# Expert blocks of 32 rows in four column groups of TensorE, turned by VectorE, with the down part one block behind

## The chip, the cores and the metric

The kernel runs on one core of one Trainium2 chip. The metric is the device time of one execution in microseconds (us). Three runs of the kernel before took 1458.22, 1455.94 and 1453.58 us, median 1455.94. One execution more was recorded by the profiler; its rows are read below. In them PE is TensorE's matmul, PEld its weight load, DVE is VectorE, ACT ScalarE, POOL GpSimd and SP SyncE, which here issues the weight loads. A "q" behind an engine's name is its sequencer.

## The reference

One step of a hybrid backbone on 512 sample and 128 prompt tokens, model width 1024, all in f32: a norm and modulation, two token mixers (an S5 scan and a gated linear recurrence), an output projection, then a mixture of 16 experts with two experts per token, and a final norm. The change is in the mixture of experts alone:

```python
    def expert_block(args):
        xe, e = args
        return (jax.nn.silu(xe @ w_gate[e]) * (xe @ w_up[e])) @ w_down[e]

    yb = lax.map(expert_block, (xb.reshape(n_blocks, MOE_BLOCK, dm), blk_expert)).reshape(-1, dm)
    y_slot = yb[dest] * wts.reshape(-1)[order][:, None].astype(x.dtype)
    return jax.ops.segment_sum(y_slot, tok, num_segments=n_tok)
```

640 tokens x 2 = 1280 rows are sorted by expert. Every expert's rows are padded to whole blocks. Each expert has three matrices of 1024 x 1024 f32, 4 MB each, 192 MB in all, and each is read once from HBM.

## The kernel before, in words

Everything up to the router (slices 1 to 21 of 40) keeps its order. From there on the program is a pipeline over blocks of MB = 64 sorted rows.

- **Routing.** VectorE counts the rows per expert, orders the experts and writes block numbers into `router_ints` (lines 1495 to 1610). Expert 0 comes first, since its weights can be loaded before the router is known; the others alternate between the largest and the smallest that are left. GpSimd scatters the rows of `h2` to `x_sorted` in HBM (L659). The first block's rows are picked by matmul (L2241) instead and need no trip through HBM.
- **PE, one block** (the loop at lines 2268 to 2294). The stationary operand is 64 columns of turned x; the weights are streamed, 256 or 512 columns at a time, in two column groups of the array side by side. `gates(s)`, eight times, does gate and up (L2222); `down(f)`, eight times, the last product (L2233). PE turns x of the next block (`turn_x`, L2212) and the activations (`turn_act`, L2228) itself, by matmul with an identity, in the middle of these. The down part of a block follows its own gate part. The trace counts two records per f32 matmul.
- **ScalarE** takes silu of the gate half (L948), copies turned activations (L951) and turned x (L936) out of PSUM, loads x of the block after next (L956) and stores y (L973). **VectorE** multiplies by the up half (L1661) and copies y (L1682).
- **Weights.** An expert is 24 pieces of 512 KB, each with a slot of its own in SBUF. SP issues the loads in a fixed order (`next_expert`, L525 to L553). For each expert 10 of the 16 gate and up pieces go to ten staging buffers (L532) and are copied by GpSimd into their slots when the last block of the expert before has used these (L673). The other six go straight to their slots behind waits on `gu_done` (L542, L544), the eight down pieces behind waits on `down_done` (L553). The last expert is loaded without staging.
- **The end.** y of all blocks but the last two comes back by gathers from `y_sorted` (L685) and is scaled and added by VectorE (L1643, L1647). The last two blocks stay in SBUF (`y_last`, L1656) and are merged by matmuls with `last_tokens_t` (L2311).

## Time and profile before

| | |
|---|---|
| median of three runs | 1455.94 us |
| span of the profiled execution | 1449.7 us |
| what lies around the span, median less span | 6.2 us |
| PE busy | 1358.5 us, 94% |
| PE weight load busy | 850.3 us, 59% |
| VectorE, ScalarE, GpSimd busy | 433.9, 265.5, 234.1 us |
| chain that ended last | PE 79%, DMA 8%, VectorE 5% |
| moved by DMA | 318.07 MB, mean 219 GB/s |

Each of the 40 slices is 36.2 us. A digit is the busy share in tenths. PE's share alone does not say whether the expert stage waits for weights; the steps of SP's loads from expert to expert and the DMA share of a stretch do.

### The profile page before, as it was taken

Reading aid. Unit: us, or ns where it says so; the run is one execution under the profiler, and the core shown is the slowest. Engines: PE = TensorE matmul, PEld = TensorE weight load, DVE = VectorE, ACT = ScalarE, POOL = GpSimd, SP = SyncE. Lnnn points to the kernel's source line nnn. Section 1 sums busy time; section 2 is a strip of 40 time slices with the busy share of each in tenths; the row PEclk is TensorE's granted clock in tenths of the full one; section 3 lists DMA queues with packets and bytes.
Section 4 is the critical chain, followed back from the end, with each engine's and each line's share of the span. In section 5 each row is a group of like instructions: output and inputs, shape, how many; then the busy total and the mean of one; then the engine's idle time right before and its main releaser. Section 6 shows DMA issues by size and latency. Waiting matters only on the chain.

```text
span 1449.7 us, 26021 instructions
## 1 busy us (share of the span) xinstructions
PE 1358.5 (94%) x10242; PEld 850.3 (59%) x10243; DVE 433.9 (30%) x913; ACT 265.5 (18%) x401; POOL 234.1 (16%) x280
## 2 busy tenths in 40 slices
PE   5898999978999999999969999999999999999975
PEld 3688778756787666664434455555555455554532
DVE  4792860375622412104462000000000000000065
ACT  3305012244125000000111111111111111111102
POOL 0043402200000000000005013003122222222320
PEclk9899899998999999999989999999999999999997
DMA  7459622345430212413168818917949999999993
GB/s 302 152 136 386 140 69 66 81 147 181 170 111 10 87 44 73 172 46 145 44 249 330 342 29 340 395 29 292 396 155 396 389 398 380 403 380 403 377 402 132
DMA packets 91756, 318.07 MB, mean 219 GB/s; under 512 B 11920, under 2 KB 12304, under 8 KB 91440
## 3 DMA queue, kind: packets, MB, share of 16 engines
q1 hardware_dynamic: 72304, 268.77, 48.9%
q0 software_dynamic: 10608, 34.19, 8.0%
q10 hardware_dynamic: 8784, 14.24, 3.2%
q8 instruction: 46, 0.75, 0.2%
q14 instruction: 14, 0.11, 0.0%
HBM read 281.99 MB, written 33.06 MB: 217 GB/s over the span
## 4 chain that ended last, share of the span: by engine, by line
PE 79%; DMA 8%; DVE 5%; issue 3%; ACT 2%; SPq 2%; POOL 0%; POOLq 0%; DVEq 0%; ACTq 0%
PE ps L2222 22%; PE ps L1762 11%; PE ps L2233 11%; PE ps L1750 10%; DMA expert_w<-in_w_down 5%; PE ps L2132 5%; PE ps L2183 4%; PE ps L1854 2%; PE ps L1937 2%; DMA expert_w<-in_w_up 2%; SPq L553 1%; PE ps L2228 1%; PE ps L2212 1%; PE ps L1777 1%; DMA x_sorted<-h,router_ints 1%
## 5 line engine op out<-in xcount | busy, mean ns | idle before, releaser
L2222 PE MATMUL ps<-expert_w,x_block_t 128*64 128x256 f32 x3584 | 405.8, 383 | 10.6 <-issue 6.7
L2222 PEld LDWEIGHTS ps<-expert_w,x_block_t 128*64 128x64 f32 x3584 | 257.2, 138 | 159.1 <-issue 33.7
L2233 PE MATMUL ps<-expert_w,act_t 128*64 128x512 f32 x896 | 212.7, 602 | 4.1 <-DMA expert_w<-in_w_down 3.7
L1762 PE MATMUL ps<-h_t,weight_ring 128*128 128x320 f32 x640 | 179.0, 436 | 0.1
L1762 PEld LDWEIGHTS ps<-h_t,weight_ring 128*128 128x128 f32 x640 | 121.6, 191 | 54.2 <-issue 7.6
L1750 PE MATMUL ps<-h_t,weight_ring 128*128 128x320 f32 x512 | 148.8, 454 | 2.8 <-ACT h_t L730 2.8
L1661 DVE TENSOR_TENSOR activations<-silu_tmp,ps 128x256 f32<-128x256 f32 x56 | 23.6, 422 | 375.7 <-ACT silu_tmp L948 375.6
L1750 PEld LDWEIGHTS ps<-h_t,weight_ring 128*128 128x128 f32 x512 | 102.0, 201 | 46.7 <-issue 9.3
L2233 PEld LDWEIGHTS ps<-expert_w,act_t 128*64 128x64 f32 x896 | 58.3, 137 | 101.4 <-issue 81.4
L673 POOL COPY expert_w<-staged 128x1024 f32<-128x1024 f32 x42 | 43.8, 1043 | 416.8 <-PE ps L2222 315.9
L1682 DVE COPY y_block<-ps 128x512 f32<-128x512 f32 x25 | 17.3, 692 | 187.5 <-PE ps L2233 187.5
L2183 PE MATMUL ps<-w_out_sb,merged 128*128 128x512 f32 x160 | 71.1, 597 | 0.7 <-DVE x L1479 0.7
L948 ACT ACTIVATE silu_tmp<-ps 128x256 f32<-128x256 f32 x56 | 21.6, 385 | 243.3 <-PE ps L2222 234.9
L659 POOL DMA_INDIRECT x_sorted<-h,router_ints x10 | 9.7, 973 | 336.0 <-DVE router_ints L1592 333.2
L673 POOL COPY expert_w<-gathered 128x1024 f32<-128x1024 f32 x56 | 57.9, 1043 | 11.5 <-DMA gathered<-in_w_gate 8.9
L948 ACT ACT_TABLE_LOAD x27 | 34.6, 1283 | 130.8 <-issue 130.8
L2183 PEld LDWEIGHTS ps<-w_out_sb,merged 128*128 128x128 f32 x160 | 29.6, 190 | 37.0 <-issue 33.9
L1777 PE MATMUL ps<-weight_ring,c_silu 128*32 128x128 f32 x768 | 27.4, 290 | 19.4 <-DMA weight_ring<-in_stream 14.7
L704 ACT ACTIVATE gates<-ps 128x640 f32<-128x640 f32 x16 | 11.3, 704 | 169.5 <-PE ps L1762 169.5
L951 ACT ACTIVATE act_t<-ps 128x256 f32<-128x256 f32 x56 | 21.5, 384 | 100.4 <-PE ps L2228 100.4
L1854 PEld LDWEIGHTS ps<-weight_ring,h_t 128*128 128x128 f32 x320 | 35.9, 192 | 0.2
L1854 PE MATMUL ps<-weight_ring,h_t 128*128 128x128 f32 x320 | 35.9, 275 | 0.0
(355 smaller groups left out, 1309.1 us busy)
## 6 DMA issues: line engine op xcount, KB each, us to landing
expert_w<-in_w_down SPq DMA_DIRECT2D x128, 512.0 KB, 13.6
weight_ring<-in_stream SPq DMA_DIRECT2D x98, 512.0 KB, 5.0
expert_w<-in_w_gate SPq DMA_DIRECT2D x58, 512.0 KB, 11.3
expert_w<-in_w_up SPq DMA_DIRECT2D x58, 512.0 KB, 12.3
staged<-in_w_gate SPq DMA_DIRECT2D x28, 512.0 KB, 13.9
gathered<-in_w_gate SPq DMA_DIRECT2D x28, 512.0 KB, 15.9
gathered<-in_w_up SPq DMA_DIRECT2D x28, 512.0 KB, 16.5
x_sorted<-zero POOLq DMA_DIRECT2D x18, 512.0 KB, 15.0
```

What stands on the lines that cost most here:

```text
L673: nc.gpsimd.tensor_copy(w_slot[3 * f + s % 2][:, :, :].rearrange("p k c -> p (k c)"), stage[s])\
L948: nc.scalar.activation(silu[:, a, :], ps[:, 2 * a, 0:256], ACT.Silu).then_inc(silu_ready, 1)
L1661: vec.tensor_tensor(acts[:, a, :], silu[:, a, :], ps[:, 2 * a + 1, 0:256], ALU.mult).then_inc(prod_ready, 1)
L1750: last = mm(pair(job)[:, a, :], w[:, k, :], h_t[:, k, a * HALF:(a + 1) * HALF], start=(k == 0), stop=(k == KD - 1))
L1762: last = mm(pair(job)[:, a, :], w[:, k, :], h_t[:, k, a * HALF:(a + 1) * HALF], start=(k == 0), stop=(k == KD - 1))
L1777: last = mm(pair_flat(job)[rows, 0, j * P:(j + 1) * P], csil[:, k, :], w[:, k, :], start=(k < 4), stop=(k >= 4))
L1854: last = mm(pair_flat(job)[:, 0, m * P:(m + 1) * P], h_t[:, k, c * P:(c + 1) * P], ring[:, slots[m], k, :], start=(k == 0), stop=(k == KD ...
L1937: last = mm(pair(job)[:, g2, i * NB + lo:i * NB + hi], lhs, rhs, start=False, stop=(i == 3 and ri == 1 and lo > 0), skip_group_check=True)
L2132: last = mm(bank(job)[:, 0:HALF], br[:, 4 * w + k, :], y[:, k, a * HALF:(a + 1) * HALF], start=(k == 0), stop=(k == 3))
L2183: last = mm(bank(job), merged[:, k, c * P:(c + 1) * P], wo[:, k, 512 * half:512 * half + 512], start=(k == 0), stop=(k == KD - 1))
L2222: last = mm(ps[MB * g:MB * g + MB, 2 * half + w, 0:256], x_blk_t[:, 2 * kp + k2, :], rows[:, at_col:at_col + 256], start=(kp == 0 and k2 = ...
L2233: last = mm(ps[MB * half:MB * half + MB, 4, :], act_t[:, 4 * (f // 4) + 2 * (f % 2) + f // 2 % 2, :], w_slot[3 * f + 2][:, 4 * half:4 * ha ...
```

## The change

A block has 32 rows. Gate and up weights are laid out so that a piece holds, for one slice of 128 of the contraction, four strips of 256 columns (128 of up, 128 of gate); four matmuls of 32 stationary columns, one per column group, stream one strip each. The down product is cut the same way. x and the activations lie on 4 x 32 partitions, and VectorE turns them with a transpose within squares of 32; PE turns nothing in the loop. The down part of a block runs behind the gate part of the next block. All 16 gate and up pieces of every expert but the first pass through 8 staging buffers and a copy of GpSimd, with the last expert no exception; the down pieces go straight to their slots. The last four blocks stay in SBUF. With these inputs the rows per expert, in the kernel's order of experts, are 61, 209, 26, 204, 29, 134, 33, 108, 36, 88, 39, 85, 49, 65, 56 and 58.

```diff
@@ -58,14 +58,19 @@
 TILE = 32
 
 EXPERTS, EGROUPS, EPG = 16, 4, 4
-MB = 64
+MB = 32
 OVER = (2 * TOK - EXPERTS) // MB
 NBLK = EXPERTS + OVER
 X_ROWS = (NBLK + 2) * MB
 Y_ROWS = NBLK * MB
 DFF = 1024
 KF = DFF // P
-STAGED = 10
+FG = 4
+GW = D // FG
+LASTN = 4
+STAGES = 8
+PIECES = 3 * KF
...
+        w_slot = [at(f"expert_w{s}", end - s * 4096, [P, D]) for s in range(PIECES)]
+        piece = [w_slot[n] for n in SLOT_OF]
...
+        stage = [at("staged0", end + 4096, [P, D])[:, :], sm[:, b_at:b_at + D]] \
+            + [at(f"staged{2 + i}", ring0 + 12288 + i * 4096, [P, D])[:, :] for i in range(3)] \
+            + [at(f"staged{5 + i}", qs0 + 5632 + i * 4096, [P, D])[:, :] for i in range(3)]
...
             first_expert(range(20, 24))
-            def next_expert(n, staged):
+            def load_piece(e, p):
+                sp.dma_start(stage[p % STAGES], w_experts[bass.ds(e, 1), p, :, :].rearrange("a p n -> p (a n)"))\
+                    .then_inc(stage_in[p % STAGES], 16)
+
+            sp.wait_ge(act_took, h2_job("L", CH - 1) + 1)
+            sp.wait_ge(route_ready, 1)
+            second = sp.value_load(rint[0:1, EXPERT + 1:EXPERT + 2], min_val=0, max_val=EXPERTS - 1)
+            for p in range(STAGES // 2):
+                load_piece(second, p)
+            sp.wait_ge(x_scattered, 16 * 2 * CH)
+            for g in range(FG):
+                sp.dma_start(x_blk[MB * g:MB * g + MB, :], x_sorted[MB:2 * MB, GW * g:GW * g + GW]).then_inc(x_blk_in, 16)
+            def load_down(b, e):
+                for f in range(KF):
+                    sp.wait_ge(down_done, b * KF + (f + 1))
+                    sp.dma_start(piece[2 * KF + f][:, :], w_experts[bass.ds(e, 1), 2 * KF + f, :, :].rearrange("a p n -> p (a n)"))\
+                        .then_inc(down_in[f], 16)
+
+            for p in range(STAGES // 2, 2 * KF):
+                if p >= STAGES:
+                    sp.wait_ge(slot_filled, 2 * KF + (p + 1 - STAGES))
+                load_piece(second, p)
+            load_down(sp.value_load(rint[0:1, START + 1:START + 2], min_val=0, max_val=NBLK), second)
+            with sp.Fori(2, EXPERTS) as n:
                 b = sp.value_load(rint[0:1, bass.ds(n + START, 1)], min_val=0, max_val=NBLK)
                 e = sp.value_load(rint[0:1, bass.ds(n + EXPERT, 1)], min_val=0, max_val=EXPERTS - 1)
...
+                for p in range(2 * KF):
+                    sp.wait_ge(slot_filled, n * (2 * KF) + (p + 1 - STAGES))
+                    load_piece(e, p)
+                load_down(b, e)
...
-            pool.sem_inc(slot_filled, STAGED)
+            for p in range(2 * KF):
+                pool.wait_ge(first_in[p], 16)
+            pool.sem_inc(slot_filled, 2 * KF)
             pool.wait_ge(route_ready, 1)
-            with pool.Fori(1, EXPERTS - 1) as n:
+            with pool.Fori(1, EXPERTS) as n:
                 b = pool.value_load(rint[0:1, bass.ds(n + START, 1)], min_val=0, max_val=NBLK)
...
+                for p in range(2 * KF):
+                    s = p % STAGES
+                    pool.wait_ge(stage_in[s], n * (16 * 2 * KF // STAGES) + 16 * (p // STAGES + 1 - 2 * KF // STAGES))
                     pool.sem_inc(stage_full, 1)
...
+                    pool.wait_ge(gu_done, b * (2 * KF) + (p + 1))
+                    pool.sem_inc(slot_free, 1)
+                    nc.gpsimd.tensor_copy(piece[p][:, :], stage[s]).then_inc(slot_filled, 1)
...
+            with act.Fori(2, NBLK) as i:
+                with act.If(i < limit):
+                    for h in range(2):
+                        act.wait_ge(gu_done, i * (2 * KF) + (h + 1) * KF)
+                        act.wait_ge(prod_ready, i * 2 + h)
+                        take_gate_half(h)
+                    act.wait_ge(xt_copied, i + 2)
                     load_x(i * MB + 2 * MB)
...
+                    act.wait_ge(y_copied, i + 1)
+                    store_y(i * MB - MB)
...
+            dve.wait_ge(picked0, 1)
+            vec.transpose(x_blk_t[:, :, :].rearrange("p k t -> p (k t)"), ps[:, 5, 0:GW]).then_inc(xt_copied, 1)
...
+            def take_prod(h):
+                vec.tensor_tensor(acts[:, h, :], silu[:, :], ps[:, h, 0:P], ALU.mult).then_inc(prod_ready, 1)
+
+            def turn_x(src):
+                vec.transpose(x_blk_t[:, :, :].rearrange("p k t -> p (k t)"), src).then_inc(xt_copied, 1)
+
+            def turn_act():
+                vec.transpose(act_t[:, :, :].rearrange("p k t -> p (k t)"), acts[:, :, :].rearrange("p h n -> p (h n)"))\
+                    .then_inc(act_ready, 1)
+
+            def copy_y():
+                vec.tensor_copy(y_blk[:, :], ps[:, 4, 0:GW]).then_inc(y_copied, 1)
+
+            for i in range(2):
+                dve.wait_ge(silu_ready, 2 * i + 1)
+                take_prod(0)
+                dve.wait_ge(silu_ready, 2 * i + 2)
+                take_prod(1)
+                dve.wait_ge(prod_ready, 2 * i + 2)
+                if i == 1:
+                    dve.wait_ge(down_done, KF)
+                turn_act()
+                if i == 0:
+                    last_picks()
+                dve.wait_ge(x_blk_in, (i + 1) * 16 * FG)
+                dve.wait_ge(gu_done, (i + 1) * 2 * KF)
+                turn_x(x_blk[:, :])
+                if i == 0:
+                    dve.wait_ge(down_done, KF)
+                    dve.wait_ge(y_stored, 16 * FG)
+                    copy_y()
+            with dve.Fori(2, NBLK) as i:
+                with dve.If(i < limit):
+                    dve.wait_ge(silu_ready, i * 2 + 1)
+                    take_prod(0)
+                    dve.wait_ge(x_blk_in, i * (16 * FG) + 16 * FG)
+                    dve.wait_ge(gu_done, i * (2 * KF) + 2 * KF)
+                    turn_x(x_blk[:, :])
+                    dve.wait_ge(silu_ready, i * 2 + 2)
+                    take_prod(1)
+                    dve.wait_ge(prod_ready, i * 2 + 2)
+                    dve.wait_ge(down_done, i * KF)
+                    turn_act()
+                    dve.wait_ge(y_stored, i * (16 * FG))
+                    copy_y()
...
+            def gate_half(h, filled):
+                for k in range(KD):
+                    filled(KD * h + k)
+                    for g in range(FG):
+                        last = mm(ps[MB * g:MB * g + MB, h, 0:GW], x_blk_t[:, k, :], piece[KD * h + k][:, GW * g:GW * g + GW],
+                                  start=(k == 0), stop=(k == KD - 1))
+                    last.then_inc(gu_done, 1)
+
+            def down(filled):
+                for f in range(KF):
+                    filled(2 * KD + f)
+                    for g in range(FG):
+                        last = mm(ps[MB * g:MB * g + MB, 4, 0:GW], act_t[:, f, :], piece[2 * KD + f][:, GW * g:GW * g + GW],
+                                  start=(f == 0), stop=(f == KF - 1))
+                    last.then_inc(down_done, 1)
...
             blocks = pe.value_load(rint[0:1, TOTAL:TOTAL + 1], min_val=EXPERTS, max_val=NBLK)
-            with pe.Fori(1, NBLK) as i:
+            own = pe.value_load(rint[0:1, 1:2], min_val=0, max_val=EXPERTS - 1)
+            pe.wait_ge(xt_copied, 2)
+            gate_half(0, lambda p: pe.wait_ge(slot_filled, own * (2 * KF) + (p + 1)))
+            pe.wait_ge(prod_ready, 2)
+            gate_half(1, lambda p: pe.wait_ge(slot_filled, own * (2 * KF) + (p + 1)))
+            with pe.Fori(2, NBLK) as i:
                 with pe.If(i < blocks):
                     e = pe.value_load(rint[0:1, bass.ds(i, 1)], min_val=0, max_val=EXPERTS - 1)
+                    before = pe.value_load(rint[0:1, bass.ds(i - 1, 1)], min_val=0, max_val=EXPERTS - 1)
                     pe.wait_ge(xt_copied, i + 1)
...
+                    gate_half(0, lambda p: pe.wait_ge(slot_filled, e * (2 * KF) + (p + 1)))
+                    pe.wait_ge(prod_ready, i * 2)
+                    gate_half(1, lambda p: pe.wait_ge(slot_filled, e * (2 * KF) + (p + 1)))
+                    pe.wait_ge(act_ready, i)
+                    pe.wait_ge(y_copied, i)
+                    down(lambda p: pe.wait_ge(down_in[p - 2 * KF], before * 16 + 16))
...
+            pe.wait_ge(act_ready, blocks)
+            pe.wait_ge(y_copied, blocks)
+            down(lambda p: pe.wait_ge(down_in[p - 2 * KF], EXPERTS * 16))
...
+    def by_group(w):
+        return w.reshape(EXPERTS, FG, KD, MB, FG, 2, P).transpose(0, 5, 2, 1, 3, 4, 6)
+
+    gate_up = np.stack([by_group(a["moe_w_up"][0]), by_group(a["moe_w_gate"][0])], axis=6).reshape(EXPERTS, 2 * KD, P, D)
+    down = a["moe_w_down"][0].reshape(EXPERTS, FG, KF, MB, D).transpose(0, 2, 1, 3, 4).reshape(EXPERTS, KF, P, D)
```

What it moves on PE. Before, in the loop over blocks: the last gate/up part of a block, then its down part with a turn of the second half of its activations in it.

```order
L2222 MATMUL ps<-expert_w_170,x_block_t 64x256 [waits gu_in7]
L2222 MATMUL ps<-expert_w_170,x_block_t 64x256
L2222 MATMUL ps<-expert_w_171,x_block_t 64x256 x2
L2222 MATMUL ps<-expert_w_170,x_block_t 64x256 x2
L2222 MATMUL ps<-expert_w_171,x_block_t 64x256 x2
L2287 ISA [waits act_ready]
L2233 MATMUL ps<-expert_w_151,act_t 64x512 [waits y_copied,dn_in0]
L2233 MATMUL ps<-expert_w_151,act_t 64x512
L2233 MATMUL ps<-expert_w_154,act_t 64x512 [waits dn_in1]
L2233 MATMUL ps<-expert_w_154,act_t 64x512
L2283 REGISTER_ALU
L2228 MATMUL ps<-constants,activations 128x128 [waits prod_ready]
```

Now, at the same place: the last two gate/up pieces of block i, then the down part of block i - 1.

```order
L2220 MATMUL ps<-expert_w_164,x_block_t 32x256 [waits slot_filled]
L2220 MATMUL ps<-expert_w_164,x_block_t 32x256 x3
L2263 REGISTER_ALU
L2220 MATMUL ps<-expert_w_152,x_block_t 32x256 [waits slot_filled]
L2220 MATMUL ps<-expert_w_152,x_block_t 32x256 x3
L2266 ISA [waits y_copied,act_ready]
L2228 MATMUL ps<-expert_w_153,act_t 32x256 [waits first_in16]
L2228 MATMUL ps<-expert_w_153,act_t 32x256 x3
L2228 MATMUL ps<-expert_w_154,act_t 32x256 [waits first_in17]
L2228 MATMUL ps<-expert_w_154,act_t 32x256 x3
```

The turns are gone from PE, every four matmuls have a wait of their own, and the down part reads the activations of the block before.

SP before, in the loop over experts: the last gate and up pieces wait for the gate part of the expert before (`gu_done`), and the down pieces follow.

```order
L542 DMA expert_w_167<-in_w_gate 128x1024
L544 DMA expert_w_168<-in_w_up 128x1024
L541 REGISTER_ALU
L542 ISA [waits gu_done]
L542 DMA expert_w_170<-in_w_gate 128x1024
L544 DMA expert_w_171<-in_w_up 128x1024
L552 REGISTER_ALU
L553 DMA expert_w_151<-in_w_down 128x1024 [waits down_done]
```

SP now, at the same place (`expert_w_153` is the first down piece):

```order
L525 ISA [waits slot_filled]
L525 DMA staged_188<-in_w_experts 128x1024
L551 REGISTER_ALU
L525 ISA [waits slot_filled]
L525 DMA staged_189<-in_w_experts 128x1024
L538 ISA
L539 ISA [waits down_done]
L539 DMA expert_w_153<-in_w_experts 128x1024
```

All sixteen gate and up loads now wait for copies (`slot_filled`), and `down_done` is the count of a down part that PE runs one block later than before.

## Rows read from the trace of the kernel before

**Rows 1.** Page, part 2: DMA share and GB/s in 40 slices.

```profile
DMA  7459622345430212413168818917949999999993
GB/s 302 152 136 386 140 69 66 81 147 181 170 111 10 87 44 73 172 46 145 44 249 330 342 29 340 395 29 292 396 155 396 389 398 380 403 380 403 377 402 132
```

**Rows 2.** Timeline of PE, one block: start us, us, engine, line, operation.

```profile
862.38 8.80 PE L2222 MATMUL ps<-expert_w,x_block_t 128*64 128x256 f32 x80
871.12 0.44 PE L2228 MATMUL ps<-constants,activations 128*128 128x128 f32 x2
871.49 5.40 PE L2222 MATMUL ps<-expert_w,x_block_t 128*64 128x256 f32 x48
876.72 1.89 PE L2233 MATMUL ps<-expert_w,act_t 128*64 128x512 f32 x8
...
878.90 2.80 PE L2233 MATMUL ps<-expert_w,act_t 128*64 128x512 f32 x12
881.63 0.66 PE L2212 MATMUL ps<-constants,x_block 128*128 128x128 f32 x4
...
884.84 8.80 PE L2222 MATMUL ps<-expert_w,x_block_t 128*64 128x256 f32 x80
```

**Rows 3.** Timeline of SP's queue: loads of down pieces for the next expert.

```profile
792.06 9.48 SPq L553 DMA_DIRECT2D expert_w<-in_w_down  x8
878.06 7.33 SPq L553 DMA_DIRECT2D expert_w<-in_w_down  x8
903.04 12.03 SPq L553 DMA_DIRECT2D expert_w<-in_w_down  x8
...
1394.04 8.62 SPq L553 DMA_DIRECT2D expert_w<-in_w_down  x8
```

**Rows 4.** Windows: stretch, its us, busy us by engine, PEclk, DMA share, GB/s.

```profile
1240.00:1248.00 8.00, 8.00 (x43) 2.78 (x40) 0.57 (x2) 0.99 (x3) 6.58 (x7) 1.00 1.03 410
1107.00:1175.00 68.00, 67.43 (x506) 36.04 (x504) 4.60 (x9) 10.26 (x18) 20.59 (x20) 1.00 1.02 393
```

**Rows 5.** Timeline of PE: four column groups, in the conditioning stage.

```profile
410.69 1.95 PE L1777 MATMUL ps<-weight_ring,c_silu 128*32 128x128 f32 x64
```

**Rows 6.** Page, part 3: ScalarE's DMA queue, packets, MB, share of 16 engines.

```profile
q10 hardware_dynamic: 8784, 14.24, 3.2%
```

**Rows 7.** Page, part 5: GpSimd's copies, busy and mean ns, idle before.

```profile
L673 POOL COPY expert_w<-staged 128x1024 f32<-128x1024 f32 x42 | 43.8, 1043 | 416.8 <-PE ps L2222 315.9
```

**Rows 8.** Timeline of SP's queue, after a stretch in which nothing was loaded.

```profile
873.68 0.33 SPq L542 DMA_DIRECT2D expert_w<-in_w_gate  x1
```

**Rows 9.** Windows around that issue.

```profile
870.00:874.50 4.50, 4.50 (x42) 2.78 (x40) 0.35 (x1) 0.39 (x1) 4.37 (x5) 1.00 0.00 0
874.50:876.00 1.50, 1.50 (x18) 1.00 (x14) 0.00 (x0) 0.00 (x0) 0.00 (x0) 1.00 0.81 295
```

**Rows 10.** Windows: stretches before and after a change of PE's granted clock.

```profile
743.00:757.00 14.00, 7.06 (x18) 2.83 (x20) 12.34 (x50) 0.00 (x0) 0.00 (x0) 0.52 1.03 411
1399.00:1405.00 6.00, 4.85 (x22) 2.73 (x24) 4.71 (x5) 0.39 (x1) 0.86 (x1) 0.50 1.02 409
1411.00:1416.00 5.00, 2.26 (x10) 0.50 (x12) 1.86 (x2) 0.05 (x1) 0.00 (x0) 0.99 1.03 409
1416.00:1419.00 3.00, 3.00 (x10) 1.06 (x12) 2.93 (x3) 0.04 (x1) 0.00 (x0) 0.50 0.73 289
```

**Rows 11.** Timeline of SP's queue: the load of the second block's rows.

```profile
783.49 1.19 SPq L565 DMA_DIRECT2D x_block<-x_sorted  x2
```

**Rows 12.** Timeline of VectorE: a scaling, the last block, the first merged chunks.

```profile
1381.98 2.48 DVE L1643 SCALAR_TENSOR_TENSOR gathered<-gathered,router_tiles,gate_row 128x1024 f32<-128x1024 f32 x2 [3.32 <-DMA gathered<-y_sorted,router_ints]
1421.89 2.81 DVE L1656 TENSOR_TENSOR y_last<-ps,gate_row 64x512 f32<-64x512 f32 x4 [2.75 <-PE ps L2233]
1433.19 2.35 DVE L1707 TENSOR_TENSOR final<-ps,x 128x1024 f32<-128x1024 f32 x2 [8.49 <-PE ps L2311]
```

**Rows 13.** Timeline of ScalarE's queue: the load of one block's rows.

```profile
1313.71 1.20 ACTq L956 DMA_DIRECT2D x_block<-x_sorted  x2
```

More of the change, by code:

```diff
@@ L244, in hybrid_step @@
+        got = [at(f"gathered{i}", qs0 + 20480 + i * 4096, [P, D])[:, :] for i in range(3)]
+        y_last = at("y_last", qs0 + 20480 + 3 * 4096, [P, 2, D])
         b_at = SMALL["b_re"][0]
[L245 to L247 removed]
@@ L325, in hybrid_step @@
         blocks_done = sem("blocks_done")
-        got_in = [sem(f"got_in{s}") for s in range(CH)]
+        got_in = [sem(f"got_in{s}") for s in range(3)]
         pick_ready = sem("pick_ready")
@@ L1648, in add_gathered @@
-                if part == 3:
+                                                  g2_row[:, 0 if c < SCH else 1, :], ALU.mult, ALU.mult))
+                else:
+                    settle()
+                    steps[0] += 1
+                    vec.tensor_tensor(x2[:, c, :], x2[:, c, :], row, ALU.add).then_inc(dve_step, 1)
                     settle()
                     vec.nop().then_inc(got_used, 1)
-            def take_last(u, cv):
-                for half in range(2):
-                    rows = slice(MB * half, MB * half + MB)
-                    last = vec.tensor_tensor(y_last[rows, u, cv, :], ps[rows, 4, :],
-                                             g2_row[rows, cv, 512 * half:512 * half + 512], ALU.mult)
-                last.then_inc(y_last_ready, 1)
```

415 lines of the change are left out of this document (129 added, 286 removed).

## Prediction

> **What bounds the kernel now.** I read the slices first [rows 1]. From slice 22 (761 us) on it is the expert stage. Its first nine slices show DMA digits between 1 and 9 with 29 to 396 GB/s, the next nine 9s with 377 to 403. So the DMA engines have slack early and none late. PE's own rows say what sets the pace early [rows 2]: a block of 64 tokens runs from 862.38 to 884.84, 22.46 us, and PE does not wait in it. SP's first load of each expert's down weights marks the step from expert to expert [rows 3]. It comes at 792.06 for the second expert and at 1394.04 for the sixteenth: 602.0 us for 14 experts. They hold 26 of the 28 blocks, 26 x 22.46 = 584 us, so PE is the limit for 97% of that stage. An expert with four blocks takes 86.0 us (792.06 to 878.06), one with one block 25.0 (to 903.04), which is less than its weights need on the DMA engines: they were fetched ahead. A pair with three blocks then takes 68 us at 393 GB/s [rows 4], where PE (67.4) and 48 pieces of weights nearly balance.
>
> **PE per block.** A gate/up record (64 columns, 256 streamed, two groups) costs (876.72 - 862.38 - 0.37 for the turn) / 128 = 109 ns, a down record (881.63 - 878.90) / 12 = 227 ns of 512 [rows 2]. With four groups half of each per 256 columns is left if all four run together: 54.6 and 57 ns. The one place with four groups today streams 128 columns, 64 records in 1.95 us [rows 5], 30.5 ns each, so they do run together. A block of 32 has 128 gate/up and 64 down records: 7.0 + 3.6 = 10.6 us. Bounds: 10.2 if the rate is exactly that of the two-group records without their gaps, 11.7 if 256 columns cost twice the 30.5. I take 10.6, from the nearer shapes. The PE transposes (2 x 0.37 + 0.59 us a block) go. No VectorE transpose stands in the trace. Its bounds are 0.35 us (VectorE takes 0.69 for 512 columns out of PSUM [rows 12], this is 256) and, in four passes, 1.4; turning x lies beside the down part one block behind (3.6 us), turning the activations beside the next gate part, so I take nothing. If one took over 3.6 us it would show 48 times.
>
> **Blocks.** Routing the given inputs with the reference gives, in the kernel's order of experts, 61, 209, 26, 204, 29, 134, 33, 108, 36, 88, 39, 85, 49, 65, 56, 58 rows. In 32s that is 2, 7, 1, 7, 1, 5, 2, 4, 2, 3, 2, 3, 2, 3, 2, 2: 48 blocks for 28. PE alone would need 48 x 10.6 = 509 us instead of 629. That is the saving on offer, 120 us.
>
> **The weights.** They stay 24 pieces of 512 KB an expert. Undisturbed the engines move 410 GB/s [rows 4]: 1.28 us a piece, 30.7 an expert. ScalarE's queue (x and y blocks) took 3.2% of the span [rows 6], 46.4 us or 1.66 for each old block of 256 packets of 2 KB. A new block has 256 packets of 1 KB: between 0.83 (by bytes) and 1.66 (by packets), I take 1.2.
>
> **The new wait.** This is the term that decides. SP issues in order: 16 gate/up pieces of expert n, then 8 down pieces, each behind a wait for the down part of the last block of expert n-1. That part now runs one block behind, after the gate/up of expert n's first block, which needs all 16 pieces. So the last staged piece must land, be copied and be used before SP may issue anything, the next expert's pieces are queued behind it, and the DMA engines run dry once per expert. The price: copy 1.04 us [rows 7]; landing and two signals 0.4; eight gate/up records 0.44; eight down records 0.44; and 1.1 from SP's issue at 873.68 [rows 8] to the first bytes (the share is 0.00 until 874.5 and 0.81 in the 1.5 us after [rows 9]). Sum 3.4 us. Those 16 records run at half clock, for in the 1.28 us between pieces PE has work for 0.44: after the stretch 1411 to 1416, in which PE waited for pieces and was busy 2.26 of 5 us, the granted clock was 0.50 [rows 10], the 1.2 GHz level. That adds 0.9: 4.3 us. Bounds: 0 (if the engines never run dry) and 6.
>
> The Trainium skill (TensorE: Matmul & The Clock Gate, "HAM oscillation — how this bites in real kernels") says that a matmul stream broken by waits for DMA is throttled again at each wait, and it speaks against splitting this work into smaller pieces. The rows above agree; without that rule the sum would be 19 us less, with it taken to the letter 22 more, both among the rivals.
>
> So an expert that is bound by its weights takes 30.7 + 4.3 + 1.2 per block: 36.2 us with one block, 37.4 with two, 38.6 with three. With four or more PE is the longer: 10.6 per block, plus 2.6 for the about 5 us at half clock until a full stream has raised it (743 to 757 was 14 us at 0.52, 1399 to 1405 six us at 0.50 [rows 10]): 45.0, 55.6 and 76.8 us for 4, 5 and 7. Only 8 pieces are staged, so after a long expert the next 16 still have to come. The sum for the second to the fifteenth expert: 2 x 36.2 + 5 x 37.4 + 3 x 38.6 + 45.0 + 55.6 + 2 x 76.8 = 629.4 us, against 602.0: **+27.4**.
>
> **Where it starts.** SP waits until the rows are scattered and asks for the second block at 783.49 [rows 11]; the engines moved 411 GB/s before that [rows 10], so this stays. Today the second block is a full one of 22.46 and SP's first down load comes at 792.06, during it. Afterwards: x lands about 787.5, gate/up of block 1 (7.0 + 2.6 at half clock) to 797, gate/up of block 2 to 805, down load at 806. The 16 pieces are there by 804 (12 of them from 786 on, 15.4 us, then a copy). **+14.0**. The first block starts some 5 us sooner, since no PE transpose and ScalarE copy stand before it, but it then waits for that x anyhow. The routing arithmetic grows by 20 block slots, under 1 us, hidden by the scatter's DMA.
>
> **The end.** From the last down load to the end it is 55.7 us today (1394.04 to 1449.7). Afterwards: down part behind 6 us, gate/up of the last block 7, then on VectorE 14 of the 20 scaled additions (1.25 us each, as in the 2.48 for two [rows 12]) and three takings of last blocks (8 x 0.35 us) among the waits, some 30 us from the first down load, 3 of waiting for gathered rows, and 16.5 from the first merged chunk (1433.19 [rows 12]) to the end: about 49. **-6.7**, worth plus or minus 6.
>
> ScalarE issues 8 DMAs a block for 4 before. Two take 1.20 us [rows 13], so 4.8, beside two activations in 10.6: it fits, and x for the block after next is asked for 3 us and lands 8 us after a gate part ends, inside 10.6. No time for it.
>
> Sum: 27.4 + 14.0 - 6.7 = +34.7 on a span of 1449.7, 1484.4. The runs' median of 1455.94 stands 6.2 above the span: **1490.6, told as 1490 us**.
>
> **Rivals.**
> 1. *The engines do not run dry* (the other side). The stall and half the x/y price go, and the experts with one to three blocks take 31.5, 32.4 and 33.2: 4.7 x 2 + 5.0 x 5 + 5.4 x 3 = 51 less, 1440 us, faster. It decides where an expert bound by weights loses under 1 us instead of 4.3 (34.7 / 10 = 3.5 to be won back). For it: the old kernel's experts run into one another at 393 GB/s with small copies in the way. Against it: SP's order.
> 2. *The clock stays up.* 2.6 x 4 + 0.9 x 10 = 19 less: 1472, still slower. For it: slices at 410 GB/s today with PE at clock 1.00. Against: rows 10.
> 3. *Four groups do not hold their rate*, or the wait ahead of every eight records (today every sixteen) costs: 11.7 us a block, on the 23 blocks of the four experts that PE bounds: +25, 1516.
> 4. *The clock stays down* for the 14 us seen at 743, the skill's rule at full price: 4.4 more on each of the four long experts, about 5 at the end: 1512.
>
> **Chances.** Forecast 0.60, own range 1478 to 1508; rival 1 0.16; rival 2 0.10; rival 3 0.08; rival 4 0.06. The range that leaves out two in ten is 1452 to 1522. About 0.3% (4.4 us) is what a measurement of this kernel can tell from no change: of rival 1 most is faster (0.13), the rest of it and a thin edge of rival 2 lie within 0.3% (0.06), all else is slower (0.81).
>
> **What would show it.** PE records at 54 to 57 ns in a full stretch and the step between blocks 10.6 us in the long experts; steps of SP's first down load near 36 to 39 us in the short ones, 77 in the long; a gap of some 4 us in the DMA share before each such load, with PE's gate/up records paced by the copies and the granted clock 0.50 there. Wrong it is if DMA shows 9s throughout, if short experts step in 32 us, or if PE waits for VectorE's transpose or for x in every block.

## The result, and the profile after

The changed kernel takes 1536.7 us (median of 4 runs, 1535.6 to 1542.1) against 1455.2 (4 runs of the kernel before): ratio 1.058, 95% interval 1.054 to 1.062, slower. The direction was forecast; the size (1490, range 1452 to 1522) was not. The profiled execution has a span of 1533.8 us, so 2.9 lie between span and median. The page's slices, which answer to [rows 1]:

```profile
PEclk9899999999999999999779978988979898888877
DMA  7368622345302114140786297188488998888873
GB/s 300 129 194 312 100 60 63 114 149 198 138 30 69 55 60 161 55 158 20 290 314 240 64 348 296 28 329 342 138 342 308 344 343 338 338 346 335 345 273 110
```

Where the kernel before moved 377 to 403 GB/s in slices 31 to 39, this one moves 335 to 346 in slices 32 to 38. Fewer bytes per time, with the same weights to fetch: something stands still in between. Four windows, in the columns of [rows 4]: one around such a gap, one over the greater part of an expert with two blocks, one in an expert with one block, and one in an expert with seven:

```profile
1426.00:1431.00 5.00, 3.67 (x64) 1.74 (x60) 0.68 (x2) 0.28 (x1) 2.08 (x2) 1.00 0.09 25
1195.00:1235.00 40.00, 32.42 (x436) 12.70 (x429) 4.11 (x12) 1.39 (x5) 17.45 (x17) 0.79 0.85 328
900.00:930.00 30.00, 18.03 (x140) 3.90 (x144) 0.95 (x3) 0.56 (x2) 16.67 (x16) 0.51 0.89 355
829.00:889.00 60.00, 55.50 (x1012) 33.04 (x1008) 8.79 (x26) 3.06 (x11) 14.07 (x15) 1.00 0.35 119
```

DMA share 0.09 for five microseconds: the engines run dry. They do so once per expert, as forecast: in the 5 us ahead of the down load at the end of each of the ten short steps the share is between 0.1 and 0.35. In the third row PE is paced by the copies (it waits for them sixteen times) and its granted clock is 0.51, next to the lower of its two levels. The fourth row is the surprise: full clock, DMA at 0.35, so nothing but PE can be the limit, and still PE is busy 55.5 of 60 us. PE's timeline shows where the rest is (answers to [rows 2]; L2220 is the gate/up part, L2228 the down part):

```profile
834.28 3.63 PE L2228 MATMUL ps<-expert_w,act_t 128*32 128x256 f32 x64
838.82 7.11 PE L2220 MATMUL ps<-expert_w,x_block_t 128*32 128x256 f32 x128 [0.91 <-issue]
845.74 3.64 PE L2228 MATMUL ps<-expert_w,act_t 128*32 128x256 f32 x64
850.27 7.11 PE L2220 MATMUL ps<-expert_w,x_block_t 128*32 128x256 f32 x128 [0.89 <-issue]
```

The records keep the forecast rate (7.11 us for 128, 3.64 for 64), but 0.9 us lie ahead of every gate part, and "issue" says that no semaphore and no DMA was waited for. A block takes 850.27 - 838.82 = 11.45 us instead of 10.6.

SP's first load of each expert's down pieces (answers to [rows 3]):

```profile
808.67 5.72 SPq L539 DMA_DIRECT2D expert_w<-in_w_experts  x8
892.62 4.40 SPq L539 DMA_DIRECT2D expert_w<-in_w_experts  x8
...
1197.09 4.42 SPq L539 DMA_DIRECT2D expert_w<-in_w_experts  x8
...
1234.66 4.95 SPq L539 DMA_DIRECT2D expert_w<-in_w_experts  x8
...
1467.27 4.51 SPq L539 DMA_DIRECT2D expert_w<-in_w_experts  x8
```

All fifteen give these steps:

| blocks of the expert | forecast, us | measured |
|---|---|---|
| 1 (two experts) | 36.2 | 37.7, 37.4 |
| 2 (five) | 37.4 | 38.8, 37.6, 38.8, 38.6, 37.6 |
| 3 (three) | 38.6 | 39.9, 38.7, 39.1 |
| 4, 5 | 45.0, 55.6 | 47.1, 60.8 |
| 7 (two) | 76.8 | 84.0, 82.7 |
| first load at | 806 | 808.7 |
| last load to the end | 49 | 66.5 |

At the end VectorE, GpSimd and PE, each from its timeline (answers to [rows 12]):

```profile
1464.91 1.04 POOL L655 COPY expert_w<-staged 128x1024 f32<-128x1024 f32 x1 [0.19 <-issue]
1466.54 1.00 POOL L664 DMA_INDIRECT gathered<-y_sorted,router_ints  x1 [0.59 <-issue]
```

```profile
1472.58 1.28 DVE L1619 SCALAR_TENSOR_TENSOR gathered<-gathered,router_tiles,gate_row 128x1024 f32<-128x1024 f32 x1 [24.74 <-DMA gathered<-y_sorted,router_ints]
...
1482.26 0.45 DVE L1641 STREAM_TRANSPOSE x_block_t<-x_block 128x256 f32<-128x256 f32 x1 [0.31 <-DVE x L1624]
```

```profile
1482.84 9.57 PE L2220 MATMUL ps<-expert_w,x_block_t 128*32 128x256 f32 x128 [12.75 <-DVE x_block_t L1641]
```

GpSimd issues its gathers only behind the last expert's sixteen copies, since that expert is staged like all others now. VectorE stood waiting for them 24.74 us with the turn of the last block's x queued behind, and PE 12.75 us for that turn.

### The profile page after: what moved, and what is told of

Same layout as the page of the kernel before. It is cut to its first block, busy times and chain, and to the rows that moved or that the text cites. A ratio compares the mean times of both kernels' runs of the same rounds, so it can differ in the third digit from the quotient of the medians.

```text
span 1533.8 us, 38078 instructions
## 1 busy us (share of the span) xinstructions
PE 1303.5 (85%) x14745; PEld 808.5 (53%) x14746; DVE 481.3 (31%) x1101; ACT 197.3 (13%) x328; POOL 333.1 (22%) x376
## 4 chain that ended last, share of the span: by engine, by line
PE 56%; DMA 15%; POOL 9%; issue 7%; DVE 6%; SPq 4%; ACT 2%; POOLq 1%; DVEq 0%; ACTq 0%
PE ps L1768 11%; DMA staged<-in_w_experts 10%; PE ps L2220 10%; PE ps L1756 9%; POOL expert_w L655 8%; PE ps L2228 5%; PE ps L2138 5%; PE ps L2189 4%; PE ps L1860 2%; SPq L539 2%; DMA expert_w<-in_w_experts 2%; PE ps L1943 2%; DMA gathered<-y_sorted,router_ints 1%; PE ps L1783 1%; SPq L525 1%
## 5 line engine op out<-in xcount | busy, mean ns | idle before, releaser
L2220 PE MATMUL ps<-expert_w,x_block_t 128*32 128x256 f32 x6144 | 416.4, 417 | 147.1 <-POOL expert_w L655 84.5
L2220 PEld LDWEIGHTS ps<-expert_w,x_block_t 128*32 128x32 f32 x6144 | 194.1, 115 | 367.9 <-POOL expert_w L655 189.5
L655 POOL COPY expert_w<-staged 128x1024 f32<-128x1024 f32 x210 | 216.5, 1043 | 442.6 <-PE ps L2220 294.9
L2228 PE MATMUL ps<-expert_w,act_t 128*32 128x256 f32 x3072 | 186.0, 394 | 13.2 <-issue 6.3
L2228 PEld LDWEIGHTS ps<-expert_w,act_t 128*32 128x32 f32 x3072 | 104.0, 114 | 88.2 <-issue 19.4
L915 ACT ACTIVATE silu_tmp<-ps 128x128 f32<-128x128 f32 x96 | 26.7, 278 | 728.3 <-PE ps L2220 691.6
L1638 DVE TENSOR_TENSOR activations<-silu_tmp,ps 128x128 f32<-128x128 f32 x96 | 27.6, 287 | 279.4 <-ACT silu_tmp L915 277.1
L2138 PE MATMUL ps<-y_s,weight_ring 128*128 128x320 f32 x128 | 35.8, 433 | 0.0
L2138 PE MATMUL ps<-y_hg,weight_ring 128*128 128x320 f32 x128 | 35.8, 433 | 0.0
L1783 PEld LDWEIGHTS ps<-weight_ring,c_silu 128*32 128x32 f32 x768 | 21.5, 116 | 25.1 <-issue 20.2
```

The lines of the kernel that those rows point to most:

```text
L655: nc.gpsimd.tensor_copy(piece[p][:, :], stage[s]).then_inc(slot_filled, 1)
L1638: vec.tensor_tensor(acts[:, h, :], silu[:, :], ps[:, h, 0:P], ALU.mult).then_inc(prod_ready, 1)
L1783: last = mm(pair_flat(job)[rows, 0, j * P:(j + 1) * P], csil[:, k, :], w[:, k, :], start=(k < 4), stop=(k >= 4))
L2138: last = mm(bank(job)[:, 0:HALF], br[:, 4 * w + k, :], y[:, k, a * HALF:(a + 1) * HALF], start=(k == 0), stop=(k == 3))
L2220: last = mm(ps[MB * g:MB * g + MB, h, 0:GW], x_blk_t[:, k, :], piece[KD * h + k][:, GW * g:GW * g + GW], start=(k == 0), stop=(k == KD - 1))
L2228: last = mm(ps[MB * g:MB * g + MB, 4, 0:GW], act_t[:, f, :], piece[2 * KD + f][:, GW * g:GW * g + GW], start=(f == 0), stop=(f == KF - 1))
```

## The experiments

Each edit is to the changed kernel, unless it says otherwise; the diffs are shortened. "Steps" are those of the table above, each read from one profiled execution. Even where nothing was edited ahead of it, SP's load of the second block's rows comes between 778.1 us (with one load later) and 788.9 us (with the leaner copies), so a few microseconds in where the expert stage starts say nothing about an edit.

**Gathers early.**

```diff
-            with pool.Fori(1, EXPERTS) as n:
+            with pool.Fori(1, EXPERTS - 1) as n:
                 ...copies of expert n
             pool.wait_ge(y_stored, limit * (16 * FG))
+            gathers 0, 1, 2
+            with pool.Fori(EXPERTS - 1, EXPERTS) as n:
+                ...copies of expert n
-            gathers 0 to 9
+            gathers 3 to 9
```

> GpSimd issues the first three of its ten gathers after the copies for the fifteenth expert and ahead of those for the sixteenth, instead of behind all sixteen of these. Nothing else changes. My theory: the end is long because VectorE waits 24.7 us for gathered rows in front of the work that turns x of the last block, so PE waits 12.75 us for that x. GpSimd idles 16.8 us before the first copy for the last expert, so the three issues (0.95 us each) cost nothing there. PE's wait for the last x falls below 2 us, the stretch from the last first-down-load to the end shrinks from 66.5 to about 53 us, the whole by 12 to 15: 1522 to 1525 us. Rival A: the gathers issued early only move the wait to the fourth one, which is still behind all copies: 3 to 6 us. Rival B: the three issues delay the first copies for the last expert, whose backlog GpSimd never recovers: the gain is under 3 us.

Measured: 1530.6 us (1522.9 to 1537.3), ratio to before 1.052 (1.047 to 1.057). That is 6 us less than 1537 by the medians, not the 12 to 15, and the two intervals overlap, so the total alone does not show a gain. The trace shows where it arises: from the last first-down-load to the end it is 56.7 us instead of 66.5, and PE no longer waits for the last x, so the cause is right; but the last step grew from 37.6 to 43.3. Rival A named 3 to 6 us too, with a wait that only moves to the fourth gather; that is not what took the rest. The gathers moved 1.57 MB on GpSimd's queue between 1440 and 1470, 3.8 us at 410 GB/s, just where the weights need the engines, and the copies were held up for their pieces:

```profile
1448.27 1.04 POOL L655 COPY expert_w<-staged 128x1024 f32<-128x1024 f32 x1 [2.02 <-DMA staged<-in_w_experts]
1450.92 1.63 POOL L655 COPY expert_w<-staged 128x1024 f32<-128x1024 f32 x1 [1.61 <-DMA staged<-in_w_experts]
```

**Four pieces ahead.**

```diff
                 for p in range(2 * KF):            # expert n, pieces AHEAD to 15 now
                     sp.wait_ge(slot_filled, ...)
                     load_piece(e, p)
+                for p in range(AHEAD):             # AHEAD = 4, expert n + 1
+                    sp.wait_ge(slot_filled, ...)
+                    load_piece(after, p)
                 load_down(b, e)
```

> SP issues the first four staged pieces of the next expert ahead of the eight down pieces of this one, so that the DMA engines have 2 MB to fetch while the down part of the last block is awaited. Same bytes, same number of DMAs. My theory: the engines run dry for 4.7 to 5 us per expert that is bound by its weights, and this is what keeps such an expert at 37.5 to 39 us instead of 30.7 plus its x and y blocks. It goes: steps of experts with 1, 2 and 3 blocks near 32, 33 and 34.5 us, ten of them by 4.5 to 5.5 each, steps of 4, 5 and 7 blocks as now: 1537 minus 42 to 52 = 1485 to 1495 us, and the DMA share shows 9s. Rival A: the pace is not the dry spell but GpSimd's copies at 1.28 us and PE at half clock behind them: steps fall by less than 2 us, 1520 or above. Rival B: with four pieces moved ahead the down pieces land later and PE waits for them in the long experts too: no gain.

Measured: 1493.9 us (1492.3 to 1501.4), ratio 1.028 (1.024 to 1.032), 43 less. Steps: 33.1 (1 block), 32.9 to 33.8 (2), 35.7 to 37.1 (3); 4, 5 and 7 blocks 47.7, 59.2, 84.2 and 82.9, as before the edit. The ten short steps sum to 343.1 us against 384.1. The first window has the times of the one that had 0.85 above (the program is some 20 us further there); the second is the 5 us ahead of the down load at 1283.71, for the one that had 0.09:

```profile
1195.00:1235.00 40.00, 32.83 (x468) 15.21 (x472) 4.25 (x13) 1.39 (x5) 16.11 (x16) 0.83 1.00 375
1279.00:1284.00 5.00, 3.96 (x56) 1.31 (x51) 0.68 (x2) 0.28 (x1) 2.90 (x3) 0.82 1.02 413
```

Bytes, order of PE's work and number of DMAs are the same, so the dry spell itself cost these 41 us: 4.1 per short expert. The clock does not explain it: in the 5 us ahead of the down loads at 1040.22 and 1213.83 it is still 0.50, and the steps that end there take 33.1 and 33.8 us.

**Both.** The two diffs together.

> Both changes together: three gathers early and four staged pieces ahead of the down pieces. My theory: they touch different stretches and add up: 1537 minus 55 to 65, 1472 to 1482 us, still slower than the kernel before (1455). If the sum is smaller than the two apart by over 5 us, the gathers stand in the way of the copies which come earlier now; if the kernel before is beaten, the boundary gap of PE and the clock are worth less than I think.

Measured: 1493.5 us, ratio 1.027 (1.024 to 1.030), the same as with four pieces alone. The end is 55.0 us instead of 66.7, but the last step is 37.9 instead of 33.6: 7 us less where the gathers can act. The start (3.3 later) and the other steps (4 longer together) take these back in the profiled execution; they lie ahead of the gathers, so the gathers did not cause it, and why the medians are equal stays open. The sum that I expected does not hold.

**The down part at once.**

```diff
-                    before = pe.value_load(...i - 1)
...
-                    pe.wait_ge(act_ready, i)
-                    pe.wait_ge(y_copied, i)
-                    down(...before * 16 + 16)
+                    pe.wait_ge(act_ready, i + 1)
+                    pe.wait_ge(y_copied, i + 1)
+                    down(...e * 16 + 16)
```

> The down part of a block runs right behind its own gate part instead of one block behind. The rest (32 tokens, four groups, turns by VectorE) stays. My theory: in experts bound by their weights the down part of the last block no longer waits for the next expert's 16 staged pieces, so SP issues without a stop and ten short experts save 4.5 to 5.5 us each (-42 to -52); in the four long experts PE waits in each of 23 blocks for product, turn and PSUM, about 1.5 us (+25 to +40): 1515 to 1530 us in sum, steps of 2 blocks near 33, of 7 blocks near 94. Rival: the lag is not what empties the DMA queues (copies or clock are): steps of 2 blocks stay at 37 to 39, and the time is 1560 or above.

Measured: 1559.5 us (1553.4 to 1566.0), ratio 1.070 (1.067 to 1.074). Steps: 30.6 and 31.1 (1 block), 31.2 to 33.6 (2), 44.2 to 46.0 (3), 58.5, 70.0, and 95.1 and 95.0 (7). The mechanism is confirmed in the short steps: without the lag an expert with two blocks takes 6 us less, and the DMA share in the 5 us ahead of the down loads of all experts with one or two blocks is 1.02 or 1.03, so it was the lag that emptied the queues. The block in a long expert:

```profile
835.63 7.11 PE L2220 MATMUL ps<-expert_w,x_block_t 128*32 128x256 f32 x128
844.47 3.66 PE L2228 MATMUL ps<-expert_w,act_t 128*32 128x256 f32 x64 [1.72 <-DVE act_t L1644]
848.19 7.11 PE L2220 MATMUL ps<-expert_w,x_block_t 128*32 128x256 f32 x128
857.02 3.66 PE L2228 MATMUL ps<-expert_w,act_t 128*32 128x256 f32 x64 [1.72 <-DVE act_t L1644]
```

A block takes 12.55 us for 11.45, 1.1 more and not 1.5. Seven make 88; 5 of the other 7 us of a step of 95 are lost in the expert's first block, whose down part now needs the down pieces at once and took 8.6 us (812.99 to 821.6) for 3.66. My total missed for three reasons: the four long steps are 44 us longer together (I had 25 to 40), the three steps of 3 blocks are 5.5 to 7 longer each and not 5 shorter, so that the ten short steps give back 25 and not 42 to 52, and the end is 20 longer, which I had not counted. In the tail, whose order is written for the lag, PE stood idle 21.68 and 8.78 us ahead of the last two down parts; the end is 86.2 us for 66.5. These rows also hold a clue: the gate part follows the down part with no gap. This variant has one register load in PE's loop where the changed kernel has two.

**Two more register loads.**

```diff
                     e = pe.value_load(...i)
                     before = pe.value_load(...i - 1)
+                    pe.value_load(...i)
+                    pe.value_load(...i - 1)
```

> In each pass of PE's block loop two more register loads from the table of blocks stand behind the two that are there (the expert of this block, for the gate and up pieces, and that of the block before, for the down pieces). They read the same words and change nothing else. My theory: the 0.9 us in which PE stands still between the down part and the next gate part in every block is made of these loads: each takes PE's sequencer a fixed time, and the 64 short down records in front (57 ns each) cover only part of it. Doubled, the gap grows from 0.9 to 2 to 2.7 us, a block in a long expert from 11.45 to between 12.5 and 13.2, and with 23 blocks bound by PE the kernel takes 25 to 45 us longer: 1560 to 1580. Rival: the gap belongs to the branch at the loop's end or to fetching the code of the next pass: it stays at 0.9 and the time at 1537.

Measured: 1580.4 us (1578.3 to 1582.2), ratio 1.088 (1.086 to 1.090), 44 more, at the upper end of the range. The gap is 2.2 us in the long experts:

```profile
843.74 7.11 PE L2220 MATMUL ps<-expert_w,x_block_t 128*32 128x256 f32 x128 [2.22 <-issue]
856.48 8.80 PE L2220 MATMUL ps<-expert_w,x_block_t 128*32 128x256 f32 x128 [2.17 <-issue]
```

Two loads added (2.2 - 0.9) = 1.3 us, 0.65 each. The second row has a gate part of 8.80 us instead of 7.11, which the first does not. The granted clock tells them apart: it is 0.63 from 856.4 to 861.0, the first half of the second row, and 1.00 from 843.74 to 851.0, the first row; in the changed kernel it stays at 1.00 from 829 to 889. So with the longer gaps some blocks lose clock too: the four long steps grew by 38 us, of which 23 x 1.3 = 30 are the gaps. Steps of 7 blocks are 94.6 and 96.1, those of 1 and 2 blocks unchanged (36.8 to 39.0).

**One load later.**

```diff
                     e = pe.value_load(...i)
-                    before = pe.value_load(...i - 1)
                     gate_half(0, ...)
                     pe.wait_ge(prod_ready, i * 2)
+                    before = pe.value_load(...i - 1)
                     gate_half(1, ...)
```

> The register load for the block before (which only the down part needs) moves from the head of PE's pass to between its two gate halves; one load stays at the head, as in the kernel before. My theory: at the head one load fits under the down records that are queued (no gap between down and gate part was seen where only one stands there), so the gap of 0.9 us falls below 0.3; in the middle 64 gate records of 55 ns are queued in front, which hide the other. A block in a long expert takes 10.6 to 10.8 us instead of 11.45, 23 blocks: 1537 minus 12 to 20 = 1517 to 1525 us. Rival: the gap only moves to the middle of the gate part (0.9 us there), or stays at the head since it is the branch's: 1537.

Measured: 1517.2 us (1513.8 to 1518.0), ratio 1.044 (1.043 to 1.046), 20 less, in the range. PE's timeline:

```profile
840.77 7.11 PE L2220 MATMUL ps<-expert_w,x_block_t 128*32 128x256 f32 x128
847.70 3.64 PE L2228 MATMUL ps<-expert_w,act_t 128*32 128x256 f32 x64
851.43 7.11 PE L2220 MATMUL ps<-expert_w,x_block_t 128*32 128x256 f32 x128
```

851.43 - 840.77 = 10.66 us a block, what the forecast had. In the profiled executions 16 us of the gain are in the four long steps. Steps of 4, 5 and 7 blocks: 46.4, 56.4, 78.0 and 77.8 (forecast 45.0, 55.6, 76.8); the short ones stay at 37.1 to 40.3.

**Copies leaner.**

```diff
-                    pool.sem_inc(stage_full, 1)
```

> GpSimd has one of its two bare semaphore instructions between the copies taken out; the two waits stand one behind the other. My theory: GpSimd copies at exactly the DMA engines' pace (1.28 us per piece, of which 1.04 is the copy), so a backlog that it has behind the first pieces is never worked off. With 0.24 between the copies lowered to about 0.17 it works off 1 us over 16 pieces: the steps of ten short experts fall by 0.5 to 1 us: 1527 to 1532 us. Rival: the pieces' arrival sets the pace and the copies only follow: 1537, no change.

Measured: 1537.6 us (1533.0 to 1540.0), ratio 1.057 (1.055 to 1.060): no change, my theory of a backlog on GpSimd falls. The interval between copies stays at 1.28 us, and the row says now what they wait for:

```profile
1231.41 1.04 POOL L654 COPY expert_w<-staged 128x1024 f32<-128x1024 f32 x1 [0.24 <-DMA staged<-in_w_experts]
1232.69 1.04 POOL L654 COPY expert_w<-staged 128x1024 f32<-128x1024 f32 x1 [0.24 <-DMA staged<-in_w_experts]
```

**Four ahead and the load later.** Both diffs.

> Four staged pieces ahead of the down pieces (which gave 1494 us) and the later register load together. My theory: with the dry spell gone experts with three blocks are bound by PE too, so the gap counts in 32 blocks instead of 23: 1494 minus 17 to 28 = 1466 to 1477 us, steps of 3 blocks 34 instead of 36.5, of 7 blocks 77 to 79 instead of 83.5; that is the 10.6 us per block and the steps without a stall, and still 10 to 20 us over the kernel before, from the start (+14) and the end (+11). Rival: clock or arrival of the pieces sets those steps as well, and nothing or little is gained.

Measured: 1479.4 us (1475.7 to 1482.0), ratio 1.018 (1.015 to 1.020), 2 above the range that I expected. Steps 32.9 (1), 34.1 to 34.4 (2), 35.5 (3), 46.0, 56.2, 79.1 and 78.5: together 603.1, against 602.0 in the kernel before. So with both costs taken out the middle of the stage is even, and the 29 us of span that remain are the start (first down load at 809.5, 17 later than 792.06 [rows 3]) and the end (66.1 for 55.7).

**Eight pieces before the scatter.** On top of that version (1479.4 us).

```diff
-            for p in range(STAGES // 2):
+            for p in range(STAGES):
                 load_piece(second, p)
             sp.wait_ge(x_scattered, 16 * 2 * CH)
```

> On top of the version with four pieces ahead and the later register load (1479 us): SP asks for all eight staged pieces of the second expert before it waits for the scattered rows, instead of four. Theory: the start costs 17 us more than before because PE has only 10 us of work in the one block of the first expert that is left, while 12 pieces have yet to arrive behind the scatter; the DMA engines stand still for about 5 us in front of 783 us. Four pieces more fill that: first down load 4 to 5 us sooner, at 804 to 806, and the kernel at 1474 to 1476. Rival: the x block that PE waits for lands behind those pieces, 3 to 5 us later: no gain, or a loss up to 4 us.

Measured: 1479.6 us, ratio 1.018 (1.015 to 1.021), no change; the rival's case. SP's load of the second block's rows comes at 789.85 instead of 783.74, 6.1 later, of which 3.3 were there already when the first staged piece was asked for; the first down load comes at 814.8 instead of 809.5. So the edit itself delayed the rows by 2.8 us, and what the pieces win is lost on them. The steps add up to 599.1 us for 603.1, which is no more than they vary (606.6 in the last version below). That the scatter is held up by them in the DMA engines is likely, and not shown apart.

**Eight ahead.** On the version at 1479.4 us again, AHEAD = 8 instead of 4.

> On top of the same version: eight staged pieces ahead of the down pieces instead of four. Theory: the queues have not run dry since four were put ahead, and what an expert with two blocks still costs above its weights (34.1 against 30.7 plus 1.7) is not a dry spell but the engines' share of full rate: 1479 plus or minus 3. Rival: four pieces (5.1 us) do not quite cover the wait, and eight save another 1 to 2 us in each of ten short experts: 1460 to 1470.

Measured: 1516.1 us (1510.9 to 1521.5), ratio 1.043 (1.038 to 1.047), 37 more, which neither theory had. The rival's saving is there, 1 to 2 us in each step of 2 blocks, but all longer steps grow. Steps of 2 blocks 32.3 to 33.1, of 3 blocks 40.4 to 41.2, of 7 blocks 83.6 and 82.6. PE's timeline in an expert of three blocks:

```profile
1240.49 0.62 PE L2242 MATMUL ps<-expert_w,act_t 128*32 128x256 f32 x8
1241.69 0.64 PE L2242 MATMUL ps<-expert_w,act_t 128*32 128x256 f32 x8 [0.58 <-DMA expert_w<-in_w_experts]
...
1248.82 2.29 PE L2242 MATMUL ps<-expert_w,act_t 128*32 128x256 f32 x16 [0.19 <-DMA expert_w<-in_w_experts]
```

The eight staged pieces stand ahead of the down pieces in SP's one queue, and the down part of this expert's first block waits for those: it takes 10.6 us (1240.49 to 1251.1) instead of 3.64. The last block's gate part, which frees the slots for the copies, is late by that, and the step grows by 5 us. In experts with one or two blocks the steps did not grow. Of the 41 us between the two profiled executions, 29.5 are in the steps and 9.3 ahead of the first down load.

**All, with the gathers early.** Four ahead, load later, eight before the scatter, gathers early.

> Four pieces ahead, later register load, eight pieces before the scatter, and three gathers ahead of the last expert's copies. Theory: the gathers win 10 us behind the last first-down-load and give back 4 to 6 before it (their 1.6 MB stand in the same DMA queues as the weights): 3 to 5 below the version without them, near 1470. Rival: as in the pair without and with them on the plain four-ahead version, nothing is left: 1475. In neither case is the kernel before (1454 to 1456) reached.

Measured: 1477.0 us (1475.4 to 1477.8), ratio 1.017 (1.014 to 1.020): the lowest of the study, by 2 us, but its runs overlap with those of the two versions at 1479, and still slower than the kernel before. No version beat that.

## Why the prediction was wrong

The direction and the new wait were right. Two terms failed: PE's time per block, in which a register load at the head of PE's pass stood at nothing, and the end. By its own sum: 1490.6 + 2.7 (start) + 29.2 (steps) + 17.5 (end) - 3.3 (2.9 around the span, where 6.2 was taken) = 1536.7.

- **PE per block, 10.6 us: the failed step in the long experts.** The rates of the records were right (55.5 and 57 ns), and so was the opinion that turns cost PE nothing in the loop (VectorE's take 0.44 us, beside the matmuls). What the sum left out was in the diff: a second register load at the head of PE's pass, for the block before. It is no matmul and I gave it no price. With it a block takes 11.45. Four long steps came out 20.3 over; moving that load took 20 us off the kernel, 16 of them in these steps, and adding two put 44 on. Of the 29 us of the steps this is two thirds. The kernel before has one load at that place and no gap there [rows 2]; the versions here with one load at the head have none either, with down records of 57 ns in front. Whether the kernel before's records of 227 ns would have hidden a second load, no run shows. I did not look for it since the instruction is not in any row of busy time. The Trainium skill (DMA: Bandwidth & Descriptors, "Latency and other measured facts") lists a floor of about 600 ns for `tensor_load`. It does not say on which engine, nor that a register load like this one is meant; the 0.65 measured here is near it.
- **The new wait, 4.3 us per expert: right.** The mechanism is shown by both undoings (four ahead: 4.1 per short expert; no lag: 6 to 7 in those with one or two blocks). The ten short steps were 8.9 us over the forecast in all, under 1 each. I took half clock for all ten. In the 5 us ahead of the down load it was 0.50 or 0.51 for three steps of 2 blocks, which took 38.6 to 38.8 us, and 1.00 for one, which took 37.6: about 1.1 us, where I had 0.9. That is read from the trace; no run changed the clock alone. The 0.4 us for landing and signals had no row behind it. At the last expert 0.05 us lie between the end of the last copy (1465.95) and PE's records (1466.00), and some 0.35 between PE's first eight down records and SP's issue at 1467.27: 0.4 for the two signals, and nothing left for the landing.
- **x and y blocks, 1.2 us each: not tested by itself.** The two 1-block steps against the five 2-block steps differ by 0.8 (38.3 - 37.5). Queue q10's share is 2.7% of the span, 41 us or 0.86 for each of 48 blocks if all that the queue carried is put on them: near the bound by bytes (0.83). The row answers to [rows 6]:

```profile
q10 hardware_dynamic: 17424, 11.90, 2.7%
```

- **Where it starts: right**, 808.7 for 806, and with it the parts: the first gate part took 9.36 us for 9.6. The second lost 2.4 us at its end in waits for the copies of the last pieces. That the sum is off by no more than 3 us is in part luck, since the load of the second block's rows alone comes between 778.1 and 788.9 in versions that change nothing ahead of it.
- **The end, 49 us: the other failed step.** I counted 14 of 20 scaled additions behind the last down load and took it that six had been done before, as in the kernel before. I missed that staging the last expert, too, puts its sixteen copies ahead of the gathers on GpSimd. All twenty fell behind, with the turn of x queued between them. With gathers early the end was 56.7, so 10 of the 17.5 us are shown to be this, though 6 of them came back in the step ahead. Of the other 8, some 2 are VectorE's taking of the last blocks, 3.47 us each where I had 2.8, three times behind the last down load; the rest stays open.
- **Rivals.** The first (no dry spell) was wrong on the facts; its text says that half the x and y price goes, its figures take off a third (0.83 for 1.2). The second and the fourth on the clock: ahead of the short experts' down loads it was 0.50 in some and up to 1.00 in others, so neither held throughout. In the four long experts 1.3 to 3.8 us were left above 11.45 per block, 2.8 in the mean, where the forecast had 2.6 and the fourth rival 7.0. The third gave 1516 for the right symptom, 11.45 against its 11.7 us a block, with the wrong cause: four groups do hold their rate.

## What to carry to other kernels

Price the register loads at the head of a loop: one was hidden behind 64 queued records of 57 ns, a second one was not, and it cost 0.9 us in every pass. A step that is delayed by one iteration delays whatever is waiting to refill its buffers, and an in-order issuer passes the wait on to everything behind it; a few transfers put ahead of the wait win it back, but as many as cover the wait and no more, since they stand ahead of the delayed ones too (4 pieces: -43 us; 8, with the load later: 1516.1 us against 1517.2 with none ahead, no gain). And when one stage is made uniform, look at the special case that it removed: the last expert had been left unstaged, and the tail depended on it.

## What the runs showed of the hardware that I had not expected

- Two more register loads at the head of PE's pass added 1.3 us to the gap ahead of the gate part, 0.65 us each, from (2.2 - 0.9) / 2. With one load there the gap is under 0.1 us behind 64 records of 57 ns, with two 0.9.
- VectorE's scalings and additions got slower while GpSimd copied. With the gathers early, one scaling took 2.16 us and one addition 1.94; in the tail, where GpSimd copied nothing, they took 1.28 and 1.22. The Trainium skill (SBUF — State Buffer, "SBUF: two separate sides") says that a VectorE operation with two inputs in SBUF and a GpSimd operation that reads SBUF lock each other out of a shared pair of ports; these rows agree: the scaling at 1448.23 overlaps with the copy at 1448.27, and the copy at 1450.92, which began while an addition ran, took 1.63 us for 1.04. No run took the copies away alone.

```profile
1448.23 2.16 DVE L1628 SCALAR_TENSOR_TENSOR gathered<-gathered,router_tiles,gate_row 128x1024 f32<-128x1024 f32 x1 [1.58 <-DMA gathered<-y_sorted,router_ints]
...
1453.66 1.94 DVE L1633 TENSOR_TENSOR x<-x,gathered 128x1024 f32<-128x1024 f32 x1
...
1473.16 1.28 DVE L1628 SCALAR_TENSOR_TENSOR gathered<-gathered,router_tiles,gate_row 128x1024 f32<-128x1024 f32 x1 [2.70 <-DMA gathered<-y_sorted,router_ints]
```
